# First attention of a two-block transformer kernel: filler tiles moved in front of and into the compressed keys' scores, and the compressed keys and values split straight out of PSUM

## What is computed

```python
kc = compress(kv[0], cmp_pos_k, w_cmp_k1, w_cmp_k2)   # 31 compressed keys per group
vc = compress(kv[1], cmp_pos_v, w_cmp_v1, w_cmp_v2)
lc = einsum('bghqd,bgcd->bghqc', q * 64**-0.5, kc)
pc = masked_softmax(lc, cmp_end[None, :] <= t[:, None])
o_c = einsum('bghqc,bgcd->bghqd', pc, vc)
...
o = gates[0] * o_c + gates[1] * o_s + gates[2] * o_w
```

## Time and profile before

| | us |
|---|---|
| Median of 3 runs | 2184.55 |
| Lowest and highest | 2181.2, 2186.37 |
| The profiled execution, whole | 2185.68 |
| Its span | 2183.9 |
| TensorE busy in it | 2146.1 (98%) |
| VectorE, ScalarE, GpSimd busy | 1013.6, 869.6, 933.8 |

### The profile page before, as it was taken

One profiled execution on the slowest core, in us unless ns is written; L12 is line 12 of the kernel. 1 busy time (PEld: TensorE's weight loads), 2 busy tenths in 40 slices (PEclk: granted clock), 3 DMA queues, 4 the chain that ended last, 5 costly groups with the idle time before them and its releaser, 6 DMA issues.

```text
span 2183.9 us, 25305 instructions
## 1 busy us (share of the span) xinstructions
PE 2146.1 (98%) x10192; PEld 1758.8 (81%) x10192; DVE 1013.6 (46%) x1637; ACT 869.6 (40%) x1358; POOL 933.8 (43%) x424
## 2 busy tenths in 40 slices
PE   9999999999999999999999999999999999999998
PEld 7877778888888887777778888888888888888886
DVE  5877775445524235666634422313653345122134
ACT  5434346444424254444434422324532244233234
POOL 5722124434444455322225444444554454444446
PEclk9999999999999999999999999999999999999999
DMA  4421112233233332211122333322223323332222
GB/s 159 148 75 41 47 49 80 94 97 106 97 97 97 97 115 78 70 57 49 49 67 88 97 97 97 97 97 87 97 87 97 97 85 99 97 97 96 97 80 85
DMA packets 53829, 193.27 MB, mean 88 GB/s; under 512 B 6096, under 2 KB 6224, under 8 KB 53712
## 3 DMA queue, kind: packets, MB, share of 16 engines
q1 hardware_dynamic: 52992, 189.81, 27.0%
q10 hardware_dynamic: 720, 1.84, 0.3%
HBM read 189.53 MB, written 2.10 MB: 88 GB/s over the span
## 4 chain that ended last, share of the span: by engine, by line
PE 89%; DVE 6%; ACT 3%; issue 1%; DMA 0%; POOL 0%; DVEq 0%; ACTq 0%; POOLq 0%
PE ps L519 27%; PE ps L521 27%; PE ps L520 27%; PE ps L733 1%; DVE ps L1209 1%; PE ps L982 1%; PE ps L713 1%; PE ps L1000 1%; PE ps L725 1%; ACT w_hi L1855 1%; PE ps L615 1%; DVE xg_lo L1169 1%; PE ps L1007 0%; DVE ps L1730 0%; PE ps L715 0%
## 5 line engine op out<-in xcount | busy, mean ns | idle before, releaser
L472 POOL TENSOR_TENSOR w_lo<-w_raw,w_hi 128x1024 fp32r<-128x1024 f32 x352 | 852.6, 2424 | 1211.4 <-ACT w_hi L1855 1211.3
L519 PE MATMUL ps<-xg_hi,w_hi 128*128 128x512 f32 x1688 | 674.1, 399 | 5.4 <-POOL w_lo L486 2.8
L521 PE MATMUL ps<-xg_hi,w_lo 128*128 128x512 f32 x1688 | 661.2, 392 | 0.0
L520 PE MATMUL ps<-xg_lo,w_hi 128*128 128x512 f32 x1688 | 660.7, 391 | 0.0
L1855 ACT ACTIVATE w_hi<-w_raw 128x1024 fp32r<-128x1024 f32 x352 | 372.3, 1058 | 626.5 <-PE ps L521 623.8
L519 PEld LDWEIGHTS ps<-xg_hi,w_hi 128*128 128x128 f32 x1688 | 318.8, 189 | 69.3 <-issue 3.0
L521 PEld LDWEIGHTS ps<-xg_hi,w_lo 128*128 128x128 f32 x1688 | 318.5, 189 | 67.9
L520 PEld LDWEIGHTS ps<-xg_lo,w_hi 128*128 128x128 f32 x1688 | 319.2, 189 | 59.4
L521 PE MATMUL ps<-h_hi,w_lo 128*128 128x512 f32 x688 | 267.8, 389 | 0.0
L519 PE MATMUL ps<-h_hi,w_hi 128*128 128x512 f32 x688 | 267.8, 389 | 0.0
L520 PE MATMUL ps<-h_lo,w_hi 128*128 128x512 f32 x688 | 267.8, 389 | 0.0
(11 more groups left out here) (342 smaller groups left out, 2462.7 us busy)
## 6 DMA issues: line engine op xcount, KB each, us to landing
w_raw<-in_weights SPq DMA_DIRECT2D x352, 512.0 KB, 3.5
out_x<-mixed SPq DMA_DIRECT2D x8, 256.0 KB, 2.1
resid<-in_x SPq DMA_DIRECT2D x3, 512.0 KB, 7.4
p_raw<-in_p ACTq DMA_DIRECT2D x3, 512.0 KB, 3.6
resid<-in_x SPq DMA_DIRECT2D x2, 256.0 KB, 4.0
last_gain<-in_last_gain SPq DMA_DIRECT2D x1, 512.0 KB, 4.6
w_raw<-in_weights SPq DMA_DIRECT2D x1, 256.0 KB, 4.0
w_raw<-in_weights ACTq DMA_DIRECT2D x1, 256.0 KB, 4.4
```

Of the source, the lines that this page charges most:

```text
L472: pool.tensor_tensor(w_lo[:, slot, :], w_raw[:, u % RAW, :], w_hi[:, slot, :].bitcast(F32), ALU.subtract).then_inc(w_ready, 1)
L519: pe.matmul(o, w, x, start=start, stop=False)
L520: pe.matmul(o, w, xl, start=False, stop=False)
L521: return pe.matmul(o, wl, x, start=False, stop=stop)
```

## The change

Four things, all in the first attention.

1. `NSA_FILL` is changed. In j = 0 the tiles go from (2, 2) in each of the four blocks to (7, 2), (2, 0), (2, 0), (2, 1). In the last block (i = 3) of the odd steps (2, 2) becomes (1, 2, 1). The totals per step stay 16.
2. Of the seven, four tiles are issued ahead of the waits for `klo` and its like, and one each behind the first three of the four groups of `cmp_scores(0)`; none stands between it and `scores(0, 0)` any more.
3. In the later `cmp_scores(p)` two tiles stand between the second and the third group, one behind them, and one (was two) in front of `values`, `turn` and the compressed scores. At j = 7, which has no compressed scores, the two follow `turn` directly.
4. `kc_f` and `vc_f` are gone. ScalarE rounds the keys out of bank 4 in two halves, one per group, VectorE masks the values in place in bank 5, and both low parts are formed from PSUM. The 32nd column of the keys is set to zero early on.

```diff
-NSA_FILL = [((2, 2),) * 4] + [((2, 2),) * 4, ((2, 2, 2), (2, 1), (2, 2), (2, 1))] * 4
+NSA_FILL = [((7, 2), (2, 0), (2, 0), (2, 1))] + [((2, 2), (2, 2), (2, 2), (1, 2, 1)), ((2, 2, 2), (2, 1), (2, 2), (2, 1))] * 4
...
-            def cmp_scores(p):
+            def cmp_scores(p, between):
...
+                    if qi < QB - 1 and between[qi]:
+                        fill(between[qi])
                 mm.then_inc(s_cs["scores"], 1)
...
+            fill(4)
             pe.wait_ge(c_act, 5)
             pe.wait_ge(s_kv["lo"], 6)
             pe.wait_ge(s_kv["zero"], 4)
-            pe.wait_ge(s_cmp["klo"], 2)
+            pe.wait_ge(s_cmp["klo"], 4)
...
-                            cmp_scores(0)
-                            fill(pieces[0])
+                            cmp_scores(0, (1, 1, 1))
                         scores(j, i)
...
                     if j % 2 and i == QB - 1 and j < 7:
-                        cmp_scores(j // 2 + 1)
+                        cmp_scores(j // 2 + 1, (0, pieces[2], 0))
+                    elif j == 7 and i == QB - 1:
+                        fill(pieces[2])
                     fill(pieces[1])
...
-            dve.memset(kc_f[:], 0.0).then_inc(s_cmp["out"], 1)
+            for t in (kc_hi, kc_lo):
+                dve.tensor_scalar(t[:, NC1:NCP], ones[:, 0:1], 0.0, None, ALU.mult).then_inc(s_cmp["out"], 1)
...
             dve.wait_ge(unit_done, U["cmp_out"] + 1)
-            dve.wait_ge(s_cmp["out"], 1)
-            dve.tensor_copy(kc_f[0:HD, 0:NC1], ps[0:HD, 4, 0:NC1]).then_inc(s_cmp["out"], 1)
-            dve.tensor_copy(kc_f[HD:P, 0:NC1], ps[HD:P, 4, NC1:2 * NC1]).then_inc(s_cmp["out"], 1)
-            dve.tensor_tensor(vc_f[:], ps[0:2 * NC1, 5, 0:P], own[:], ALU.mult).then_inc(s_cmp["out"], 1)
+            dve.tensor_tensor(ps[0:2 * NC1, 5, 0:P], ps[0:2 * NC1, 5, 0:P], own[:], ALU.mult).then_inc(s_cmp["out"], 1)
             dve.memset(token[:, 12:13], 0.0).then_inc(bank_free, 1)
             dve.wait_ge(s_cmp["khi"], 2)
-            dve.wait_ge(s_cmp["out"], 4)
-            low(kc_lo[:], kc_f[:], kc_hi[:], s_cmp["klo"])
-            low(vc_lo[:], vc_f[:], vc_hi[:], s_cmp["klo"])
+            for g in range(2):
+                rows = slice(g * HD, (g + 1) * HD)
+                low(kc_lo[rows, 0:NC1], ps[rows, 4, g * NC1:(g + 1) * NC1], kc_hi[rows, 0:NC1], s_cmp["klo"])
+            dve.wait_ge(s_cmp["khi"], 3)
+            dve.tensor_tensor(vc_lo[:], ps[0:2 * NC1, 5, 0:P], vc_hi[:].bitcast(F32), ALU.subtract).then_inc(s_cmp["klo"], 2)
...
-            act.wait_ge(s_cmp["out"], 4)
-            copy_hi(kc_hi[:], kc_f[:], s_cmp["khi"])
-            copy_hi(vc_hi[:], vc_f[:], s_cmp["khi"])
+            act.wait_ge(unit_done, U["cmp_out"] + 1)
+            for g in range(2):
+                rows = slice(g * HD, (g + 1) * HD)
+                copy_hi(kc_hi[rows, 0:NC1], ps[rows, 4, g * NC1:(g + 1) * NC1], s_cmp["khi"])
+            act.wait_ge(s_cmp["out"], 3)
+            copy_hi(vc_hi[:], ps[0:2 * NC1, 5, 0:P], s_cmp["khi"])
```

More of the change, by code:

```diff
@@ L278, in build @@
             vv_lo = sb("vv_lo", [P, 2, 2, QB, P], F32R, att)
-            kc_f = sb("kc_f", [P, NCP], scope=att)
             kc_hi = sb("kc_hi", [P, NCP], F32R, att)
             kc_lo = sb("kc_lo", [P, NCP], F32R, att)
-            vc_f = sb("vc_f", [2 * NC1, P], scope=att)
             vc_hi = sb("vc_hi", [2 * NC1, P], F32R, att)
```

## The result

The changed kernel takes **2195.54 us** (median of 18 executions, 2185.72 to 2199.72); the kernel before took 2184.86 beside it. The ratio is 1.0038, with a 95% interval of 1.0029 to 1.0047 (the ratio of the medians alone would be 1.0049, that of the means, 2193.25 against 2184.70, 1.0039): slower by 0.4%, where no measurable change was forecast (2183.3, range to 2188.2). The 18 times stand in two groups with nothing between them: six from 2185.72 to 2186.86, with a mean granted clock of 0.996 or 0.997, and twelve from 2195.12 to 2199.72, at 0.989 to 0.992. The profiled execution is one of the lower group (2185.72 us, span 2184.0). So there are two things to explain: why the lower group gained nothing over before, and what the upper group's further 10 us are.

What follows compares the result with a forecast made beforehand. The prediction took TensorE, busy 98% of the span, as the bound, with only its idle time and clock to gain from. From 2185.68 us, -2.85 (first phase), +3.54 (later places) and -3.08 (clock) gave 2183.3, range 2178.5 to 2188.2.

Steps and rivals of the forecast that it cites:

- Part one: Splitting keys and values out of PSUM: short subtractions, low parts done near 123.8 us instead of 127.58.
- Rival (c): The split gets no quicker: `klo` still comes at 127.5, TensorE waits 1.2 us behind its four tiles, 2184.5 us; chance 0.08.
- Part two: Four tiles ahead of the first mask run 123.61 to 126.33 us; the 4.06 us idle is gone.
- Part three: Single tiles between groups of the first compressed scores cost 0.98 us each; TensorE idles 1.1, `scores(0,0)` begins at 132.15.
- where this gain goes: First phase: VectorE's chain sets its end; window branch at 148.13 instead of 150.98, gain 2.85 us, 3.3 wait before `scores(0,3)`.
- Rival (a): VectorE's chain does not bind; the first phase ends near 143.5 by TensorE's own work, total 2178.7 us; chance 0.17.
- Part four: Three later compressed scores: wait grows from 0.52 to 1.2 us, 1.18 lost at each place, 3.54 us in all.
- Rival (d): The later places cost nothing, changes and waits included, and the clock falls are gone: 2179.8 us; chance 0.12.
- Part five: Later compressed scores at p = 1 and p = 3: both clock falls prevented, 1.54 us each, 3.08 us back.
- the stretch without full tiles: At the later masks, turns, idle and small matmuls: 0.4, 0.5, 1.8 us become 0.4, 1.2, 1.0; shorter, so falls prevented.
- Rival (b): Idle time drops the clock at four places (before `scores(0,3)`, three later compressed scores), 1.54 us each: 2189.5 us; chance 0.10.
- The sum: Whole kernel: 2185.68 (profiled execution) - 2.85 + 3.54 - 3.08 = 2183.3 us, 1.3 below the median of 2184.55.

Runs made afterwards that it cites:

- run 2: The kernel before with only the split of keys and values out of PSUM, old fill table: 2176.16 us, ratio 0.9959.
- Run 10: The changed kernel with zero products filling the waits: 22 ahead of `scores(0,3)`, 5 ahead of each later mask: 2186.88 us, ratio 1.0009.
- run 1: The changed kernel measured again with no edit: 2198.46 us, ratio 1.0058.
- run 3: The changed kernel with the odd steps put back to (2, 2), no tile inside the later compressed scores: 2186.76 us, ratio 1.0012.
- run 11: The changed kernel with 5 zero products ahead of each later mask only, the wait before `scores(0,3)` left idle: 2187.24 us, ratio 1.0009.
- run 7: The kernel before plus the split alone, with one tile moved from behind the later compressed scores to ahead, (3, 1): 2176.61 us, ratio 0.9969.
- run 5: The kernel before plus the split alone, with one tile moved from ahead of the later compressed scores to behind, (1, 3): 2178.51 us, ratio 0.9976.
- run 4: The kernel before with only the odd steps changed to (1, 2, 1), split and first phase as before: 2189.73 us, ratio 1.0019.
- run 9: The kernel before plus the split alone and the changed kernel's odd steps (1, 2, 1): 2181.54 us, ratio 0.9988.

## Why the prediction was wrong, step by step

- **Part one (the split)** was right in its durations and is the one part of the change that pays. Two key halves took 0.41 us together, `vc_lo` 0.28; done at 123.31, half a microsecond earlier than forecast, 0.40 of it because this execution reached the end of `gates` that much earlier. Rival (c) is out. The Trainium skill (SBUF — State Buffer, "Who interferes with whom") calls the port that VectorE and GpSimd share an exclusive lock; VectorE's ends at 126.04 and 140.91, each within 0.3 us of the end of GpSimd's instruction, agree with it. What part one missed is the comparison that would have judged the rest: alone it brings the whole gain, 8.7 us (run 2), because `klo` then comes with the end of `gates` and there is no idle time for four tiles to fill.
- **Part two (four tiles in front)** had its times right (mask at 125.93, forecast 126.33, which is the same 0.40) and its worth wrong. I counted the gap of 4.06 us as filled by the tiles; the split had closed it already, and the tiles only delay what follows.
- **Part three and "where this gain goes"**: `scores(0,0)` at 131.66 (forecast 132.15), the idle 0.96 (1.1), the second maximum at 135.49 (136.09). Then the step to the third maximum took 7.45 us, forecast 5.39. **This is the step that failed first**: I took VectorE's instructions between the two maxima at their old durations, and moved only `query_scaled` into them. Moving seven tiles ahead also completes a unit earlier and so frees the weights' ring earlier. ScalarE's `w_hi` comes at 137.13 instead of 146.44, and GpSimd's `w_lo`, 147.57 before, falls on the compressed product: +2.06. The next two steps took 0.68 and 1.09 more at half clock. -0.60 + 2.06 + 0.68 + 1.09 = +3.23: the window branch at 151.36, forecast 148.13. The wait in front of `scores(0,3)` grew with it, to 5.3 us from a forecast of 3.3. Run 10, whose clock did not fall there, took 3.89 and 2.76 us for the last two steps, as forecast (3.90 and 2.75), so these two terms are the clock. I had used the lock to price what the change removed, and did not look for where it would strike next.
- The whole first phase against run 2, where the same step took 4.79 us, adds up: `scores(0,0)` 3.72 later (4.73 counted from the end of `gates`, which run 2 reached 1.01 us later), the product 2.06, `query_scaled` 0.60, the clock 1.77, together 8.15 of the 8.14 us measured. Rival (a) is out: VectorE's chain does bind, and whatever stands ahead of `scores(0,0)` shifts it.
- **Part four (later places)** was nearly right: 1.00 us a place (4.36 against 3.36, and the same in the distances from mask to mask), not 1.18; there was no wait for the subtraction, because two tiles stand behind the scores. The wait of 1.2 us came as forecast, three times. Rival (d) is out.
- **Part five (the clock)** was right in the profiled execution alone: both falls were gone, 1.6 us each. As a forecast of the median it failed, in two ways. A fall is not 1.54 us: it lasts 3.4, 6.8 or 10.2 us at half clock here, so it costs some 1.5 to 5 us. And I took the falls as prevented because "the stretch without full tiles" got shorter; by the numbers given it went from 2.7 to 2.6 us, and the idle time in it more than doubled. The traces show falls behind these masks with a wait of 1.2 us, with 0.5 and with none. Rival (b) named this mechanism and its sign; it got 0.10, at a price of 1.54 for each of four places and so 2189.5, where twelve of eighteen executions stand at 2195 to 2199. The range held the lower group and missed the median. **This is the step that put the median out of the range.**
- The Trainium skill (TensorE: Matmul & The Clock Gate, "Why this matters for your kernels") warns of idle gaps between bursts, and I let it point at the gap in front of `scores(0,3)`. At that gap the traces agree: four of four fell in it, and the one with it filled did not. But it was not what set the times: filling it moved the median by nothing measurable, and filling three waits of 1.2 us took the upper group away.
- The sum, term by term in the profiled execution of the lower group: +0.38 for the forecast -2.85, +3.00 for +3.54, some -3.2 for -3.08, so 2185.68 + 0.38 + 3.00 - 3.2 = 2185.9, measured 2185.72. The sum also started from the profiled execution and was then set beside the median, which is 1.1 us lower; for a median it forecast 2182.2.

What stays open: why the same program falls five times in one execution and once in another. TensorE's waits were the same in both; the one with falls behind the later masks had one at 133 us as well, and whether one brings the others was not settled. One thing did differ: of the five traces with the changed kernel's first phase, the three that fell at 133 us (runs 1, 3 and 10) had reached the end of `gates` at 124.3 to 124.5 us, the two that did not (after, run 11) at 123.0 and 123.2. No run tests whether that decides.

Runs 10 and 11 show that the upper group goes when the later masks' waits are filled. They do not show how: single falls come without these waits (runs 7 and 10) and stay away with them (run 5), and low clocks come in runs 4 and 9 as well. Why 16 of 22 in the changed kernel, no run tells: what it has beyond run 9 is the later start and the waits of the first phase. By the ratios the odd steps cost 0.0019 on the kernel before (run 4), 0.0026 in the changed kernel (less run 3) and 0.0029 on run 2 (run 9), 4 to 6 us; by run 1, whose four executions were all of the upper group, it would be 0.0046, 10 us. Some 3 us of it are the 1.00 us a place at full clock; the rest is the falls, less those that the old order had.

## What to carry to other kernels

When a change closes a gap in two ways at once, price each alone: here the quicker split closed it, and the tiles meant to fill it pushed back the chain that sets the phase's end. Moving filler work forward also moves what its completion releases, such as the next weights' split; look for where that lands beside VectorE's instructions with two SBUF inputs. Where one program's times stand in groups, look at the clock of every execution, price a fall by the longest one that a trace shows, and profile more than one execution. A few zero products in a wait that exists anyway did not delay the mask behind it here, and took the slow group away; they did not keep the clock up in every execution.

## What the runs showed of the hardware

- The granted clock falls for 3.4, 6.8 or 10.2 us at a time in the attention, to 0.50, and one program's times stand in two groups 9 us apart, with a mean clock of 0.996 to 0.997 in the one and 0.989 to 0.992 in the other.
- All 13 falls between 160 and 330 us in 14 traces begin 1.3 to 3.4 us behind the mask ahead of 24 matmuls of 32 columns: 5 at 15 places with a wait of 1.2 us, 5 at 15 with 0.5 us, 3 at 12 with none.
- With three waits of 1.2 us at these masks 16 of 22 executions were in the upper group, with zero products in the waits 0 of 22. A wait of 5.3 us in front of matmuls of 512 columns brought a fall in four of four traces and cost 1.77 us; filling it changed no median measurably.
- A VectorE instruction with two SBUF inputs (128x248, 0.42 us) that meets a GpSimd subtraction took 2.48 us and ended 0.27 us behind it. Whether the two meet can hang on less than the traces resolve: `vc_lo` took 2.47 us in one kernel and 0.28 in another, starting 2.34 and 2.35 us behind the start of the same pair of GpSimd instructions.
